# The masked-product inverse of a linear-attention chunk: turning by VectorE in place of TensorE products

## The chip, the cores and the metric

One Trainium2 chip, one of its NeuronCores. The metric is the device time of one execution in microseconds. A core has five engines with queues of their own: TensorE (PE: matmuls, with PEld loading weights), VectorE (DVE), ScalarE (ACT), GpSimd (POOL) and SyncE (SP, here the queue of the weight loads). They are kept in order by semaphores that the kernel waits on by hand.

## What is computed

A decoder trunk of two layers on 512 tokens of width 1024, all in float32. Layer 0 has a feed-forward block, a mixer (sliding-window attention beside RWKV-7), a second feed-forward block and a gated embedding; layer 1 the same with forgetting attention. Only the RWKV-7 part of layer 0 is touched by the change. It has 8 heads of width 64, and the reference runs it token by token:

```python
def step(state, inp):
    r_t, w_t, k_t, v_t, kk_t, a_t = inp
    s_kk = jnp.einsum('bhij,bhj->bhi', state, kk_t)
    state = (state * w_t[:, :, None, :]
             - s_kk[..., None] * (kk_t * a_t)[:, :, None, :]
             + v_t[..., None] * k_t[:, :, None, :])
    return state, jnp.einsum('bhij,bhj->bhi', state, r_t)
```

## The kernel before

The kernel works in chunks of C = 64 tokens (NC = 8 chunks). Within a chunk the recurrence becomes products with the inverse of a unit triangular 64x64 matrix, I + A, where A is made of the masked products of `b` and `kk`. There are 8 heads x 8 chunks = 64 such matrices. They are treated in two passes, `h` = 0 and `h` = 1 (heads 0 to 3, heads 4 to 7), and each pass in two halves, `q` = 0 and 1. A half is one 128x512 tile: two matrices on top of each other (64 partitions each), eight side by side. So one operation of VectorE, GpSimd or ScalarE on a half is 128x512, and one "group" of TensorE is 16 products 64x64x64 in float32, which the profile shows as 32 instructions.

The inverse grows by doubling: level 0 inverts blocks of 2x2, then each level 1 to 5 (LEVELS = 6) doubles the blocks. Both the inverse M (`m_x[:, q, 0]`) and its transpose (`mt_inv`) are kept, since TensorE contracts over the partitions. One level is:

- `a_level` (GpSimd, L2462): the part of A that this level joins, `a_lev = am0 * mask`.
- `xs` (TensorE, through the helper at L1894): X = the product of `a_lev` and M, one group a half.
- `x_copied` (ScalarE, L2126): X from PSUM to `m_x[:, q, 1]`.
- `ms` (TensorE): `mx`, the correction of M, and `mxt`, the correction of its transpose, one group each a half. At level 5 only `mxt`.
- `level_done` (VectorE, L2263 and L2268): `m_x[:, q, 0] -= mx`, `mt_inv -= mxt`.

The start of a pass: `ab` and `ak` (TensorE, L1881) make the pair products; `ab_masked` (VectorE, L2230) writes `am0` and `am2`, `ak_masked` (L2243) writes `akm`. Then TensorE turns `am0` by products with `eye` (`aab`), VectorE masks the result from PSUM (L2252) and subtracts it from the unit matrix (L2256): M of level 0. GpSimd makes the transposed start from `am0` alone (L2440, L2444) and then `diag` (L2451). `f` (TensorE, needs `akm`) is copied by ScalarE (`f_copied`, L2119).

Each engine's order is written out by hand. Between the levels of pass 0 stands the front of pass 1 (`front[0]` to `front[10]`): `lora_w` (its bank is freed by `f_copied`), the sigmoid `sig_w` with a table load (L1703), the scan `lc` (L1747), `lcm` (L1751), and so on; also `late[0]`, two mixes (L1496). Between the levels of pass 1 stands the tail of pass 0: `yz` (TensorE, waits for both `f_copied` of pass 1), `y_raw` (L2297), `gn_squared`, `gn_summed` (L2309), `g` (L2035), `g_copied`, `gn_std` with a table load (L2171), `gn_normed` (L2320), `y_turned`, `y_weighted`, `y_lows` (L2336). Behind the last level come `w_and_e`, `gq`, `hs`, `yc`, and the chain of states.

The helper `seen` makes an engine wait for the step of that name, pass and half; `level_seen` the same for a level; `turn_seen` for steps whose halves come in the other order in pass 0.

Of the kernel before, what the change touches and what calls it, by code (L numbers as in the profile page):

```python
# [71 lines left out]
    "pair_products": "ab ak aab f", "pair_masks": "ab_masked ak_masked init m0", "inverse_start": "mt_masked mt0 diag",  # L72
    "f_copied": "f_copied", "a_level": "a_level", "x": "x", "x_copied": "x_copied", "mx": "mx", "mxt": "mxt",
# [32 lines left out]
def trunk(nc, dram, out, stages=STAGES):  # L106

    ctx = ExitStack()
    with ctx:
# [165 lines left out]
        masks = view("masks", [P, 9, C])  # L275
# [924 lines left out]
        rwkv_fills = 56  # L1200
# [374 lines left out]
        MASK_T, MASK_TI, MASK_0, MASK_LT = 0, 1, 2, 3  # L1575
# [290 lines left out]
        def rwkv_tensor(pe, st):  # L1866
# [68 lines left out]
            def aab(h):  # L1935
                for q in range(2):
                    turn_seen(pe, "ab_masked", h, q)
                    tokens_to_tokens(rb(q, 0), [(lambda j, t: am0[h][t, q, j], lambda j, t: eye[t])]
                                     ).then_inc(R["aab"], 1)

# [6 lines left out]
            def xs(h, level):  # L1947
                for q in range(2):
# [5 lines left out]
                    tokens_to_tokens(rb(q, 2), [(lambda j, t: a_lev[t, q, j], lambda j, t: m_x[t, q, 0, j])]  # L1954
                                     ).then_inc(R["x"], 1)

            def ms(h, level):
                for q in range(2):
# [5 lines left out]
                    if level + 1 < LEVELS:  # L1964
                        tokens_to_tokens(rb(q, 3), [(lambda j, t: mt_inv[t, q, j], lambda j, t: m_x[t, q, 1, j])]
                                         ).then_inc(R["mx"], 1)
                    else:
                        pe.sem_inc(R["mx"], 1)
                    tokens_to_tokens(rb(q, 0), [(lambda j, t: m_x[t, q, 1, j], lambda j, t: mt_inv[t, q, j])]
# [79 lines left out]
            aab(0)  # L2049
            f(0)  # L2050
            front[0]()
            xs(0, 1)
# [30 lines left out]
            aab(1)  # L2083
            f(1)
            xs(1, 1)
# [28 lines left out]
        def rwkv_scalar(act, st):  # L2114
# [6 lines left out]
            def x_copied(h, level):  # L2121
                for q in range(2):
                    level_seen(act, "x", h, level, q)
                    if level > 1:
                        level_seen(act, "mxt", h, level - 1, q)
                    nc.scalar.copy(m_x[:, q, 1], by_chunk(rb(q, 2)[:])).then_inc(R["x_copied"], 1)  # L2126
# [53 lines left out]
            front[0]()  # L2180
            f_copied(0)
            front[1]()
            x_copied(0, 1)
# [12 lines left out]
            yc_copied(0)  # L2196
            f_copied(1)
            x_copied(1, 1)
# [925 lines left out]
```

## Time and profile before

| | |
|---|---|
| median of 3 runs | 2134.8 us (2132.43 to 2135.35) |
| the profiled execution | 2133.81 us, its span 2131.9 us |
| TensorE busy | 2090.7 us, 98% of the span |
| VectorE busy | 1437.8 us, 67% |
| ScalarE busy | 849.9 us, 40% |
| GpSimd busy | 751.3 us, 35% |
| matmuls over L1894 in the chain of waits | 3% of the span |

The two passes of the inverse with what stands between them run from 511 to about 647 us of the span. A timeline row is: start, duration, engine, line, operation, output<-input, count, and in brackets the idle time of the engine before it with what ended it. Several like instructions in a row are merged; they overlap a little, so a merged duration is less than the sum. The row of a group of instructions by line gives the shortest, median and longest duration in ns. Granted clock 1.00 is 2.4 GHz, 0.50 is 1.2 GHz.

### The profile page before, as it was taken

Reading aid. Unit: us, or ns where it says so; the run is one execution under the profiler, and the core shown is the slowest. Engines: PE = TensorE matmul, PEld = TensorE weight load, DVE = VectorE, ACT = ScalarE, POOL = GpSimd, SP = SyncE. Lnnn points to the kernel's source line nnn. Section 1 sums busy time; section 2 is a strip of 40 time slices with the busy share of each in tenths; the row PEclk is TensorE's granted clock in tenths of the full one; section 3 lists DMA queues with packets and bytes.
Section 4 is the critical chain, followed back from the end, with each engine's and each line's share of the span. In section 5 each row is a group of like instructions: output and inputs, shape, how many; then the busy total and the mean of one; then the engine's idle time right before and its main releaser. Section 6 shows DMA issues by size and latency. Waiting matters only on the chain.

```text
span 2131.9 us, 37887 instructions
## 1 busy us (share of the span) xinstructions
PE 2090.7 (98%) x15232; PEld 1811.5 (85%) x15232; DVE 1437.8 (67%) x1748; ACT 849.9 (40%) x1152; POOL 751.3 (35%) x646
## 2 busy tenths in 40 slices
PE   8999999999989999999999999999999999999998
PEld 7989898777887899999788899987776689998977
DVE  7847576679756865656778575766666677575764
ACT  6434243454233433333344342434444344343434
POOL 2233244547433223233443141433333322323343
PEclk9999999999999999999999999999999999999999
DMA  5333333321003333343343343424323232433332
GB/s 159 89 109 103 101 86 88 89 61 40 4 4 100 99 90 109 92 117 85 96 116 89 92 117 89 119 70 111 88 79 89 79 99 80 119 88 107 89 93 89
DMA packets 366507, 192.95 MB, mean 91 GB/s; under 512 B 11038, under 2 KB 363408, under 8 KB 366368
## 3 DMA queue, kind: packets, MB, share of 16 engines
q1 hardware_dynamic: 364128, 185.11, 30.9%
q0 software_dynamic: 2224, 5.86, 0.9%
q8 instruction: 103, 1.69, 0.3%
q14 instruction: 36, 0.29, 0.0%
q10 hardware_dynamic: 16, 0.00, 0.0%
HBM read 188.81 MB, written 2.13 MB: 90 GB/s over the span
## 4 chain that ended last, share of the span: by engine, by line
PE 88%; DVE 7%; ACT 2%; issue 1%; DMA 0%; POOL 0%; ACTq 0%; DVEq 0%; SPq 0%; POOLq 0%
PE bank L468 13%; PE bank L470 13%; PE bank L469 12%; PE bank L633 11%; PE bank L634 11%; PE bank L635 11%; PE bank L1894 3%; PE bank L2544 2%; DVE w_lo L458 2%; PE bank L2546 2%; PE bank L2545 2%; PE bank L1246 1%; PE bank L1248 1%; PE bank L1247 1%; PE bank L2561 1%
## 5 line engine op out<-in xcount | busy, mean ns | idle before, releaser
L458 DVE TENSOR_TENSOR w_lo<-w_raw,w_hi 128x2048 fp32r<-128x2048 f32 (+3 forms) x192 | 393.3, 2049 | 137.9 <-ACT w_hi L453 136.9
L453 ACT CAST w_hi<-w_raw 128x2048 fp32r<-128x2048 f32 (+3 forms) x192 | 281.6, 1467 | 386.7 <-PE bank L635 164.8
L619 POOL TENSOR_TENSOR sums<-w_raw 128x512 f32<-128x512 f32 x68 | 94.9, 1395 | 778.5 <-DMA w_raw<-in_ffn_w_gu_dram 521.6
L468 PE MATMUL bank<-h_hi,w_hi 128*128 128x512 f32 x704 | 275.4, 391 | 2.2 <-DVE w_lo L458 1.9
L469 PE MATMUL bank<-h_hi,w_lo 128*128 128x512 f32 x704 | 274.2, 389 | 0.0
L470 PE MATMUL bank<-h_lo,w_hi 128*128 128x512 f32 x704 | 274.0, 389 | 0.0
L975 DVE SCALAR_TENSOR_TENSOR x<-bank,x 128x512 f32<-128x512 f32 (+1 forms) x96 | 66.3, 690 | 166.8 <-PE bank L470 166.1
L468 PEld LDWEIGHTS bank<-h_hi,w_hi 128*128 128x128 f32 x704 | 132.2, 188 | 35.0 <-issue 5.2
L633 PE MATMUL bank<-t_hi,s_hi 128*128 128x256 f32 x544 | 154.5, 284 | 1.7 <-issue 1.7
L470 PEld LDWEIGHTS bank<-h_lo,w_hi 128*128 128x128 f32 x704 | 132.2, 188 | 27.6
L469 PEld LDWEIGHTS bank<-h_hi,w_lo 128*128 128x128 f32 x704 | 132.2, 188 | 26.3
L633 PE MATMUL bank<-xn_hi,w_hi 128*128 128x256 f32 x544 | 154.4, 284 | 0.0
L633 PE MATMUL bank<-t_hi,w_hi 128*128 128x256 f32 x544 | 154.0, 283 | 0.0
L634 PE MATMUL bank<-t_hi,w_lo 128*128 128x256 f32 x544 | 154.0, 283 | 0.0
L635 PE MATMUL bank<-t_lo,s_hi 128*128 128x256 f32 x544 | 153.9, 283 | 0.0
L634 PE MATMUL bank<-xn_hi,w_lo 128*128 128x256 f32 x544 | 153.9, 283 | 0.0
L635 PE MATMUL bank<-t_lo,w_hi 128*128 128x256 f32 x544 | 153.9, 283 | 0.0
L634 PE MATMUL bank<-t_hi,s_lo 128*128 128x256 f32 x544 | 153.9, 283 | 0.0
L635 PE MATMUL bank<-xn_lo,w_hi 128*128 128x256 f32 x544 | 153.9, 283 | 0.0
L468 PE MATMUL bank<-xn_hi,w_hi 128*128 128x512 f32 x328 | 129.6, 395 | 1.6 <-DVE w_lo L458 1.0
L470 PE MATMUL bank<-xn_lo,w_hi 128*128 128x512 f32 x328 | 127.7, 389 | 0.0
L469 PE MATMUL bank<-xn_hi,w_lo 128*128 128x512 f32 x328 | 127.7, 389 | 0.0
(388 smaller groups left out, 5455.9 us busy)
## 6 DMA issues: line engine op xcount, KB each, us to landing
w_raw<-in_ffn_w_gu_dram SPq DMA_DIRECT2D x176, 512.0 KB, 5.1
w_raw<-in_ffn_w_down_dram SPq DMA_DIRECT2D x128, 256.0 KB, 3.1
w_raw<-in_ffn_w_down_dram SPq DMA_DIRECT2D x64, 192.0 KB, 3.2
w_raw<-in_even_w_in_dram SPq DMA_DIRECT2D x40, 256.0 KB, 3.3
w_raw<-in_ple_w_gate_dram SPq DMA_DIRECT2D x16, 512.0 KB, 3.7
w_raw<-in_fox_w_in_dram SPq DMA_DIRECT2D x16, 512.0 KB, 5.0
w_raw<-in_even_w_out_dram SPq DMA_DIRECT2D x16, 256.0 KB, 3.6
w_raw<-in_fox_w_in_dram SPq DMA_DIRECT2D x16, 256.0 KB, 4.3
```

The costliest lines, as they stand in the source:

```text
L453: nc.scalar.copy(w_hi[slot][:, 0:tiles], w_raw[slot][:, 0:tiles]).then_inc(w_hi_ready, 1)
L458: nc.vector.tensor_tensor(w_lo[slot][:, 0:tiles], w_raw[slot][:, 0:tiles], w_hi[slot][:, 0:tiles].bitcast(F32), ALU.subtract).then_inc(w_r ...
L468: nc.tensor.matmul(dst, w[0], hi[:, k], start=k == 0, stop=False)
L469: nc.tensor.matmul(dst, w[1], hi[:, k], start=False, stop=False)
L470: last = nc.tensor.matmul(dst, w[0], lo[:, k], start=False, stop=k == tiles - 1)
L619: nc.gpsimd.tensor_tensor(sums[:, 0:4], w[:, 8:12], w[:, 12:16], ALU.add).then_inc(sums_made, 1)
L633: nc.tensor.matmul(dst, w[0][:, k], b[0][:, k], start=k == 0, stop=False)
L634: nc.tensor.matmul(dst, w[1][:, k], b[0][:, k], start=False, stop=False)
L635: last = nc.tensor.matmul(dst, w[0][:, k], b[1][:, k], start=False, stop=k == 3)
L975: return nc.vector.scalar_tensor_tensor(x[:, ds(j)], bank[2 * slot][:], 0.5, x[:, ds(j)], ALU.mult, ALU.add)
L1894: mm = nc.tensor.matmul(dst[of_chunk(c), at:at + C], lhsT(j, of_chunk(c)), rhs(j, of_chunk(c)), start=k == 0, stop=k == len(operands) - 1)
L2544: nc.tensor.matmul(dst, hi, xn_hi[:, k], start=k == 0, stop=False)
```

## The change

TensorE no longer turns `am0`, and `mx` is no longer computed. VectorE makes `mt_inv` of level 0 from `am0` (mask, subtract), and M from `mt_inv` by a transpose in 32x32 blocks, at the start and behind the subtraction of levels 1 to 4. Up to there every block of M that isn't zero lies in a 32x32 block on the diagonal. GpSimd loses `start_inverse`, and one mask goes with its six fills. `xs` and `ms` change banks. In the hand-written orders `start_inverse` comes ahead of `ak_masked` on VectorE, `xs(h, 1)` ahead of `f` on TensorE, and `x_copied(h, 1)` ahead of `f_copied` on ScalarE.

```diff
-            def aab(h):
-                for q in range(2):
-                    turn_seen(pe, "ab_masked", h, q)
-                    tokens_to_tokens(rb(q, 0), [(lambda j, t: am0[h][t, q, j], lambda j, t: eye[t])]
-                                     ).then_inc(R["aab"], 1)
...
-                    tokens_to_tokens(rb(q, 2), [(lambda j, t: a_lev[t, q, j], lambda j, t: m_x[t, q, 0, j])]
+                    tokens_to_tokens(rb(q, 0), [(lambda j, t: a_lev[t, q, j], lambda j, t: m_x[t, q, 0, j])]
...
-                    if level + 1 < LEVELS:
-                        tokens_to_tokens(rb(q, 3), [(lambda j, t: mt_inv[t, q, j], lambda j, t: m_x[t, q, 1, j])]
-                                         ).then_inc(R["mx"], 1)
-                    else:
-                        pe.sem_inc(R["mx"], 1)
-                    tokens_to_tokens(rb(q, 0), [(lambda j, t: m_x[t, q, 1, j], lambda j, t: mt_inv[t, q, j])]
+                    tokens_to_tokens(rb(q, 2), [(lambda j, t: m_x[t, q, 1, j], lambda j, t: mt_inv[t, q, j])]
...
-            aab(0)
+            xs(0, 1)
             f(0)
             front[0]()
-            xs(0, 1)
...
-            aab(1)
+            xs(1, 1)
             f(1)
-            xs(1, 1)
             yz(0, 0)
...
             front[0]()
+            x_copied(0, 1)
             f_copied(0)
             front[1]()
-            x_copied(0, 1)
...
+            x_copied(1, 1)
             f_copied(1)
-            x_copied(1, 1)
...
+            def blocks_turned(q):
+                return nc.vector.transpose(m_x[:, q, 0].rearrange("p j t -> p (j t)"),
+                                           mt_inv[:, q].rearrange("p j t -> p (j t)"))
...
             def start_inverse(h):
                 for q in range(2):
-                    seen(dve, "aab", h, q)
+                    turn_seen(dve, "ab_masked", h, q)
                     if h:
                         seen(dve, "yc", 0, q)
-                    nc.vector.tensor_tensor(m_x[:, q, 1], by_chunk(rb(q, 0)[:]), over_chunks(masks[:, MASK_0]),
-                                            ALU.mult).then_inc(R["init"], 1)
-                for q in range(2):
-                    seen(dve, "init", h, q)
-                    nc.vector.tensor_tensor(m_x[:, q, 0], over_chunks(eye[:]), m_x[:, q, 1], ALU.subtract
-                                            ).then_inc(R["m0"], 1)
+                    nc.vector.tensor_tensor(mt_inv[:, q], am0[h][:, q], over_chunks(masks[:, MASK_LT]), ALU.mult
+                                            ).then_inc(R["mt_masked"], 1)
+                for q in range(2):
+                    seen(dve, "mt_masked", h, q)
+                    nc.vector.tensor_tensor(mt_inv[:, q], over_chunks(eye[:]), mt_inv[:, q], ALU.subtract
+                                            ).then_inc(R["mt0"], 1)
+                for q in range(2):
+                    seen(dve, "mt0", h, q)
+                    blocks_turned(q).then_inc(R["m0"], 1)
 
             def level_done(h, level):
                 for q in range(2):
+                    level_seen(dve, "mxt", h, level, q)
+                    if level == 1:
+                        seen(dve, "mt0", h, q)
+                    nc.vector.tensor_tensor(mt_inv[:, q], mt_inv[:, q], by_chunk(rb(q, 2)[:]), ALU.subtract
+                                            ).then_inc(R["mt"], 1)
+                    level_seen(dve, "mt", h, level, q)
                     if level + 1 < LEVELS:
-                        level_seen(dve, "mx", h, level, q)
-                        nc.vector.tensor_tensor(m_x[:, q, 0], m_x[:, q, 0], by_chunk(rb(q, 3)[:]), ALU.subtract
-                                                ).then_inc(R["m"], 1)
-                    level_seen(dve, "mxt", h, level, q)
-                    if level + 1 == LEVELS:
+                        blocks_turned(q).then_inc(R["m"], 1)
+                    else:
                         dve.sem_inc(R["m"], 1)
-                    nc.vector.tensor_tensor(mt_inv[:, q], mt_inv[:, q], by_chunk(rb(q, 0)[:]), ALU.subtract
-                                            ).then_inc(R["mt"], 1)
...
             ab_masked(0)
+            start_inverse(0)
             ak_masked(0)
-            start_inverse(0)
             late[0]()
...
             ab_masked(1)
+            start_inverse(1)
             ak_masked(1)
-            start_inverse(1)
...
             a_level(0, 1)
-            start_inverse(0)
             diag(0)
...
             a_level(1, 1)
-            start_inverse(1)
             diag(1)
```

## Rows read from the trace of the kernel before

**Rows 1.** The page: each engine's busy us, share of the span, instructions.
```profile
PE 2090.7 (98%) x15232; PEld 1811.5 (85%) x15232; DVE 1437.8 (67%) x1748; ACT 849.9 (40%) x1152; POOL 751.3 (35%) x646
```
**Rows 2.** Stretches of 10 us in pass 0 and pass 1; columns in the first line.
```profile
core 0: us, PE busy (x) PEld busy (x) DVE busy (x) ACT busy (x) POOL busy (x), PEclk, DMA share, GB/s
...
535.00:545.00 10.00, 10.00 (x228) 9.92 (x227) 10.00 (x18) 1.43 (x3) 6.18 (x5) 0.79 0.01 2
...
595.00:605.00 10.00, 10.00 (x372) 10.00 (x363) 7.08 (x13) 2.68 (x5) 6.54 (x6) 1.00 0.02 5
```
**Rows 3.** Timeline of VectorE at the start of pass 0; columns as told above.
```profile
515.77 2.47 DVE L2243 TENSOR_TENSOR akm<-bank,masks 128x512 f32<-128x512 f32 x4
518.16 1.27 DVE L2252 TENSOR_TENSOR m_x<-bank,masks 128x512 f32<-128x512 f32 x2
519.36 2.52 DVE L2256 TENSOR_TENSOR m_x<-eye,m_x 128x512 f32<-128x512 f32 x2
...
525.16 2.06 DVE L1747 TENSOR_TENSOR_SCAN act_in<-chunk_start,kr 128x512 f32<-128x512 f32 x1
...
529.06 1.69 DVE L1751 TENSOR_TENSOR kr<-act_in,kr 128x512 f32<-128x512 f32 x1
```
**Rows 4.** Timeline of TensorE in pass 0: `aab`, `f`, and `xs` of level 2.
```profile
515.93 2.06 PE L1894 MATMUL bank<-eye,am 64*64 64x64 f32 x64
517.82 2.03 PE L1894 MATMUL bank<-vtok,akm 64*64 64x64 f32 x64
...
533.17 3.68 PE L1894 MATMUL bank<-m_x,a_lev 64*64 64x64 f32 x64 [2.58 <-DVE m_x L2263]
```
**Rows 5.** Timeline of VectorE at the start of pass 1.
```profile
587.31 2.47 DVE L2243 TENSOR_TENSOR akm<-bank,masks 128x512 f32<-128x512 f32 x4
```
**Rows 6.** Timeline of TensorE in pass 1: last `ab`/`ak`, then `xs` and `ms`.
```profile
583.53 1.98 PE L1881 MATMUL bank<-kr,bk 64*64 64x128 f32 x64 [0.20 <-DVE am L2290]
...
591.90 1.15 PE L1894 MATMUL bank<-m_x,a_lev 64*64 64x64 f32 x32 [0.92 <-DVE m_x L2256]
...
598.73 2.00 PE L1894 MATMUL bank<-m_x,a_lev 64*64 64x64 f32 x62
...
601.06 1.13 PE L1894 MATMUL bank<-m_x,mt_inv 64*64 64x64 f32 x32
...
604.80 2.06 PE L1894 MATMUL bank<-m_x,a_lev 64*64 64x64 f32 x64
```
**Rows 7.** The chain that ended last, pass 1: start, length, what.
```profile
609.41 1.28 ACT L2171
...
624.84 0.69 DVE mt_inv L2268
```
**Rows 8.** Instructions by line, VectorE: shortest, median, longest ns, starts.
```profile
L2268 DVE TENSOR_TENSOR mt_inv<-mt_inv,bank x20: 672/678/689, 532.9 to 625.4; 128x512 f32<-128x512 f32 x20
...
L1757 DVE TENSOR_SCALAR bk<-tmp,vecs x4: 471/473/1261, 478.2 to 537.5; 128x512 f32<-128x512 f32 x4
```
**Rows 9.** Timeline of GpSimd: two maskings, two subtractions, two of `diag`.
```profile
515.93 2.50 POOL L2462 TENSOR_TENSOR a_lev<-am,masks 128x512 f32<-128x512 f32 x2 [1.61 <-DVE am L2230]
...
521.30 3.40 POOL L2444 TENSOR_TENSOR mt_inv<-eye,mt_inv 128x512 f32<-128x512 f32 x2
...
594.52 2.05 POOL L2451 TENSOR_TENSOR kr<-eye,chunk_end 128x512 f32<-128x512 f32 x2
```
**Rows 10.** Timeline of ScalarE behind `f_copied` of pass 0.
```profile
520.50 1.28 ACT L1703 ACT_TABLE_LOAD   x1
```
**Rows 11.** Timeline of TensorE: its longest other wait in the stage.
```profile
658.01 0.50 PE L468 MATMUL bank<-y_hi,w_hi 128*128 128x512 f32 x1 [3.04 <-DVE y_lo L2336]
```
**Rows 12.** Stretches of 1 us where the clock came back (columns as rows 2).
```profile
538.00:539.00 1.00, 1.00 (x25) 1.00 (x24) 1.00 (x1) 0.00 (x0) 1.00 (x1) 0.50 0.00 0
539.00:540.00 1.00, 1.00 (x35) 1.00 (x34) 1.00 (x2) 0.00 (x0) 1.00 (x2) 0.86 0.07 16
...
662.00:663.00 1.00, 1.00 (x6) 0.84 (x5) 0.94 (x2) 0.79 (x1) 0.22 (x1) 0.92 0.94 249
```

More of the change, by code:

```diff
@@ L71 @@
     "front_tails": "a_decayed b_tail k_tail masks_scaled",
-    "pair_products": "ab ak aab f", "pair_masks": "ab_masked ak_masked init m0", "inverse_start": "mt_masked mt0 diag",
-    "f_copied": "f_copied", "a_level": "a_level", "x": "x", "x_copied": "x_copied", "mx": "mx", "mxt": "mxt",
+    "pair_products": "ab ak f", "pair_masks": "ab_masked mt_masked mt0 m0 ak_masked", "diag": "diag",
+    "f_copied": "f_copied", "a_level": "a_level", "x": "x", "x_copied": "x_copied", "mxt": "mxt",
     "m": "m", "mt": "mt",
@@ L274, in trunk @@
         swa_rcp = view("swa_rcp", [P, 2, NB])
-        masks = view("masks", [P, 9, C])
+        masks = view("masks", [P, 8, C])
         eye = view("eye", [P, C])
@@ L1199, in trunk @@
         FIRST_WINDOW, APART = 27, 22
-        rwkv_fills = 56
+        rwkv_fills = 50
         hb_diff = [(prod, act_out, sq, sq_sum)[i] for i in (0, 1, 2, 3, 0, 1, 2, 3, 2, 3, 0, 1)]
@@ L1573, in chunk_seen @@
             e.wait_ge(R[name], 2 * (h * (NC - first) + c - first) + q + 1)
-        MASK_T, MASK_TI, MASK_0, MASK_LT = 0, 1, 2, 3
+        MASK_T, MASK_TI, MASK_LT = 0, 1, 2
         def turn_seen(e, name, h, q):
@@ L2125, in x_copied @@
                         level_seen(act, "mxt", h, level - 1, q)
-                    nc.scalar.copy(m_x[:, q, 1], by_chunk(rb(q, 2)[:])).then_inc(R["x_copied"], 1)
+                    nc.scalar.copy(m_x[:, q, 1], by_chunk(rb(q, 0)[:])).then_inc(R["x_copied"], 1)
             def we_copied(h):
@@ L2422, in rwkv_constants @@
                 select(m, ALU.is_ge, -k, [[0, blocks], [1, 2 * k]], 0)
-            m = masks[:, MASK_0].rearrange("p (b t) -> p b t", t=2)
-            select(m, ALU.is_ge, -1, [[-2, C // 2], [0, 2]], 1)
-            select(m, ALU.is_ge, 1, [[2, C // 2], [0, 2]], -1)
-            select(m, ALU.is_ge, 0, [[0, C // 2], [-1, 2]], 0)
             assert filled[0] == rwkv_fills
@@ L2433, in rwkv_pool @@
         def rwkv_pool(pool, st):
-            def start_inverse(h):
-                for q in range(2):
-                    turn_seen(pool, "ab_masked", h, q)
-                    if h:
-                        seen(pool, "we", 0, q)
-                    nc.gpsimd.tensor_tensor(mt_inv[:, q], am0[h][:, q], over_chunks(masks[:, MASK_LT]), ALU.mult
-                                            ).then_inc(R["mt_masked"], 1)
-                for q in range(2):
-                    seen(pool, "mt_masked", h, q)
-                    nc.gpsimd.tensor_tensor(mt_inv[:, q], over_chunks(eye[:]), mt_inv[:, q], ALU.subtract
-                                            ).then_inc(R["mt0"], 1)
             def diag(h):
```

## The prediction

> **What bounds the kernel now.** Read the page first: TensorE is busy for 98% of the span [rows 1], so a matmul saved looks like time saved. That share is an average, so the second view is the table of stretches over the inverse (511 to 625 us, both passes; pass 0 handles heads 0 to 3, pass 1 heads 4 to 7). In pass 0 TensorE and VectorE are both busy for all 10 us; in pass 1 TensorE is, VectorE for 7.1 of 10 [rows 2]. The timelines then say who waits. At the start of each pass it is VectorE: it runs without a hole from 511 to 562 us (the rows between those of [rows 3]), and TensorE fills its wait with the turning (`aab`) and with `f` [rows 4]. From 533 to 564 us the two are nearly tied. In pass 1 VectorE again sets the start [rows 5]; then TensorE is nearly continuous from one level to the next [rows 6], except where the normalisation of pass 0 (through ScalarE and VectorE) and later its `y_lows` stand ahead on VectorE [rows 7]. All that is gained or lost there moves the end of the stage, since nothing of the next stage's bulk can run before.
>
> **What is removed.** TensorE loses `aab` (64 instructions, 1.9 us in each pass [rows 4]) and `mx` of levels 1 to 4: two groups of 32 at 0.94 us, so 1.87 us a level, 7.5 us a pass (four groups make the 3.73 us from the start of `ms` to the next `xs`, 601.06 to 604.80 in [rows 6]). Together 18.8 us of its busy time. GpSimd loses four operations a pass, about 6 us (the two subtractions 3.40 us, two maskings like those of `a_level` 2.50 us [rows 9]). The six mask fills fewer lie near 360 us, with TensorE full; I cost them at nothing.
>
> **The new operation.** No 32x32 turning by VectorE is in this trace. It reads 128x512 from one place and writes as many. The nearest rows are the subtractions it replaces, 0.68 us [rows 8]; below stands the one-input TENSOR_SCALAR of L1757 at 0.47 us [rows 8], above the scan at 2.0 us [rows 3]. I take 0.68, since the subtraction is the operation nearest in form and size, and keep 0.47 and 2.0 for the range. Issued back to back such an operation costs 0.60 us, but the turning needs the subtraction just ahead of it complete, so the pair costs 0.68 + 0.68. The Trainium skill ("Vector Engine (DVE) Microarchitecture Reference", section 3.8) says that the transposing front end sustains one element per cycle and lane; no run here shows that yet, and by it my value would stand.
>
> **The start is the dear part.** VectorE's first step took the product from PSUM (0.675 us each, L2252) and one subtraction on SBUF. Now the masking reads `am0` and `masks`, both in SBUF, like the subtraction. What such an operation costs beside a busy GpSimd is in [rows 3]: the two of L2256 took 2.52 us, the two of L1751 3.4 us, against 1.27 us for the two of L2252; and in [rows 9] two of GpSimd's on this shape take 2.05 us alone and 3.40 us beside L2256. They look as if they took turns, instruction by instruction. The Trainium skill ("GPSIMD Engine Reference", section 1) says the two engines contend when VectorE has two SBUF inputs; the rows agree. The turning has one input and would be spared. `a_level` and `diag` of GpSimd still run here, so four operations of 0.58 us alternate with four of GpSimd of 1.25, 1.25, 1.04 and 1.04 us, of which about three fall between: 4 x 0.58 + 3.3 = 5.6 us (bounds 2.4 clear, 7.0 at L2256's longest). Then two turnings, 1.3 us, and only now `ak_masked`, 2.4 us [rows 5]. So `ak_masked` ends 9.3 us after `ab_masked`; before it ended after 2.4 us, and the start of the inverse after 6.1 us.
>
> **Pass 0.** `ab_masked` ends at 515.8. `xs(0,1)` can start at 522.4 (before: 521.7). `ak_masked` ends at 525.4, so `f` ends at 526.4 at the full clock; then `f_copied`, `lora_w`, the table load of 1.28 us that stands behind `f_copied` on ScalarE [rows 10], and the sigmoid: the scan `lc` could start at 529.1 us, and it started at 525.16. So 3.9 us of wait appear on VectorE, where none was. Then there is relief: GpSimd, 4 operations shorter, is out of the way when the two of L1751 run (3.3 us become 1.2): -2.1. Net +1.8 us when VectorE reaches level 1. From there it is VectorE's own list that counts: the same 2 operations a half and level, the pair 0.1 us longer (8 pairs, +0.8), and +0.5 at level 5, where `b_turned` is behind a later `xs`. That is +3.1 us. The 5.6 us of matmuls saved in levels 2 to 4 buy nothing, since VectorE was full there and stays so.
>
> **Pass 1.** The four plus two operations end at 594.2, the first turning at 593.6; `xs(1,1)` starts at 593.7, before at 591.90. But `f` now runs behind it and needs `ak_masked` (596.6), `yz(0,0)` waits for both `f_copied`, and `ms(1,1)` is queued behind `yz(0,0)` on TensorE. At full clock `f` ends at 597.7, the copy at 598.4, `yz` at 599.0, the first product of `ms` at 600.0; subtraction and turning bring `xs(1,2)` to 601.5 against 598.73 [rows 6]: +2.8. Level 2 to 3: `xs` to `x_copied` to `ms` to the pair now runs one after the other; VectorE also has `y_raw` and `gn_summed` ahead of the pair: 6.75 us for 6.07, +0.7. Level 3 to 4: the old period is `g`, table load, `gn_normed`, then the subtraction [rows 7]; `xs` of the second half waits for its turning, and the turning is behind the subtraction: +0.95. Level 4 to `w_and_e`: here the old period was TensorE's and 1.9 us go, but `y_weighted` and `y_lows`, still ahead of the last subtraction, start later: net -0.6. Sum +3.9.
>
> **The clock.** TensorE's granted clock falls twice in the whole old trace, from 2.4 to 1.2 GHz (1.00 to 0.50), both times in or just behind a wait: 2.58 us [rows 4] and 3.04 us [rows 11]. It came back 5.8 and 4.1 us after work resumed [rows 12]; the 64 matmuls that met it took 3.68 us, not 2.0 [rows 4]. With `aab` gone and `f` moved, TensorE has nothing from 516.1 to 522.4 us in pass 0, and from 585.5 (end of `ak`, [rows 6]) to 593.7 in pass 1: 6.3 and 8.2 us. So I expect both to cost. Pass 0: `xs` 3.8 us, then `f` to 528.8; the scan starts at 531.8, not 529.1, +2.7, of which I keep 2.5. Pass 1: `xs` to 597.2, `f` to 600, `yz` to 601.3, so `xs(1,2)` at 603.75: +2.2 more. A third hole, 616.6 to 620 us, opens before `xs(1,4)`: +1.4. The clock thus adds 6.1 us: 5.6 in pass 0 and 7.5 in pass 1 in all. The Trainium skill ("TensorE: Matmul & The Clock Gate", Part 1) has idling throttle the array and activity release it, which speaks against taking filler matmuls away; the rows agree.
>
> **Sum.** 13.1 us on the profiled execution of 2133.8 us (span 2131.9) gives 2146.9; that execution is 1.0 us under the median of the three runs, 2134.8, so 2147.9 us, said as 2148.
>
> **Rivals.** (1) The clock holds, or its cost hides behind VectorE: +7.0, 2142 us. For it: pass 0 has slack on TensorE; against it, the two falls. (2) The turning is dear. At 1.2 us, ten turnings in pass 0 (VectorE full) cost 5 us more and seven on pass 1's path 4 us: 2157; at the scan's 2.0 us 2170. Only the replaced row's likeness speaks against it. (3) The other side: TensorE's queue is what each level waits for. The chain of waits goes over matmuls from 595 to 609 us and from 613 to 622 us, and over nearly all of 533 to 564. If VectorE gets from a product to the next `xs` in less than the 1.87 us that the removed products took, and the masked steps are near their clear price of 0.6 us, the savings stand: 7.5 us in pass 1 and 5.6 in pass 0, 2122 us. The point that decides is whether VectorE has idle time ahead of each level; it had in pass 1, not in pass 0. (4) Gain and loss cancel: turning near 0.47 us, GpSimd out of step with the masked steps (-3 us a pass), no low clock: 2134.
>
> **How the numbers follow.** Forecast (clock falls, turning 0.68 us) 0.48; rival 1 0.17; rival 2 0.13; rival 3 0.14; rival 4 0.08. A comparison of this kernel tells about 0.2% (4.3 us) from no change; the forecast and rivals 1 and 2 lie above it: less a hundredth at the edge of rival 1, slower 0.77; most of rival 4 and that edge, same 0.08; rival 3 and a rest of rival 4, faster 0.15. The range leaves out rival 3's centre and the upper part of rival 2: 2131 to 2163; the forecast alone would be 2142 to 2154.
>
> **What would show it.** The turnings in the profile at 0.6 to 0.75 us each; TensorE idle for 6 and 8 us ahead of the first `xs` of each pass, with a clock of 0.50 behind it; VectorE waiting some 4 to 6 us for the sigmoid before the first scan of pass 0; `xs(1,2)` some 5 us later within its pass; the time from the first `ab_masked` to `w_and_e` longer by about 6 and 7 us. I am wrong if GpSimd no longer slows VectorE at the start, if the turning's time is far from 0.68 us, or if VectorE had room in pass 0 that the trace doesn't show.

## The result and the profile after

| | kernel before | changed kernel |
|---|---|---|
| median of 6 executions | 2134.76 us (2132.43 to 2137.49) | 2145.07 us (2142.78 to 2145.98) |
| ratio to before | 1 | 1.0043, 95% interval 1.0033 to 1.0053 |
| span of the profiled execution | 2131.9 us | 2143.5 us |

The change makes the kernel 10.3 us slower by the medians; the ratio gives 9.2 us (7.0 to 11.3). Forecast were 13.1 us. It takes 18.8 us of matmuls off TensorE and still loses. The page of the changed kernel (columns as in [rows 1]):

```profile
PE 2079.7 (97%) x14592; PEld 1799.0 (84%) x14592; DVE 1437.8 (67%) x1752; ACT 849.6 (40%) x1152; POOL 736.5 (34%) x632
```

All 640 matmuls are gone, but busy time fell by 11.0 us only: the rest of the 18.8 came back as matmuls at half clock. VectorE's total is the same to the tenth by chance: in the stage it is 2.8 us more (94.6 for 91.8), since the new operations are dearer, and behind the stage, on code that the change leaves alone, it is 2.8 us less (988.4 for 991.1). The stretches of the changed kernel over pass 0, pass 1 and one of [rows 2], columns in the first line:

```profile
core 0: us, PE busy (x) PEld busy (x) DVE busy (x) ACT busy (x) POOL busy (x), PEclk, DMA share, GB/s
511.00:575.00 64.00, 49.78 (x1206) 42.97 (x1208) 53.61 (x74) 22.49 (x42) 27.59 (x20) 0.92 0.01 3
575.00:640.00 65.00, 46.53 (x1362) 43.17 (x1354) 37.99 (x73) 16.74 (x34) 20.02 (x16) 0.89 0.01 3
...
595.00:605.00 10.00, 7.55 (x174) 7.47 (x176) 4.64 (x8) 2.35 (x4) 2.91 (x3) 0.61 0.01 2
```

TensorE, full in 595 to 605 us before [rows 2], is busy for 7.55 of 10 us at a mean clock of 0.61, and VectorE for 4.64 where it had 7.08: each has time in which it waits for the other. VectorE at the start of pass 0, in the timeline of the changed kernel (start, length, what; in brackets the idle time ahead and who ended it), answers to [rows 3]:

```profile
515.83 2.36 DVE L2243 TENSOR_TENSOR mt_inv<-am,masks 128x512 f32<-128x512 f32 x2
518.11 3.19 DVE L2247 TENSOR_TENSOR mt_inv<-eye,mt_inv 128x512 f32<-128x512 f32 x2
521.23 1.29 DVE L2212 STREAM_TRANSPOSE m_x<-mt_inv 128x512 f32<-128x512 f32 x2
522.45 2.44 DVE L2234 TENSOR_TENSOR akm<-bank,masks 128x512 f32<-128x512 f32 x4
...
531.17 1.22 DVE L1747 TENSOR_TENSOR_SCAN act_in<-chunk_start,kr 128x512 f32<-128x512 f32 x1 [3.52 <-ACT kr L1703]
532.31 1.20 DVE L1747 TENSOR_TENSOR_SCAN other<-chunk_start,kr 128x512 f32<-128x512 f32 x1
533.43 0.67 DVE L1751 TENSOR_TENSOR kr<-act_in,kr 128x512 f32<-128x512 f32 x1
534.01 0.68 DVE L1751 TENSOR_TENSOR kr<-other,kr 128x512 f32<-128x512 f32 x1
```

The four masked steps (two of L2243, two of L2247) take 5.4 us from 515.83 to 521.23; `ak_masked` comes 6.7 us later than in [rows 3]; the scan waits 3.52 us for ScalarE's sigmoid. GpSimd beside it in the changed kernel answers to [rows 9], the two `a_level` at 1.72 us each and the two of `diag` at 1.47 us, where two of `diag` alone took 2.05 us:

```profile
515.87 3.44 POOL L2441 TENSOR_TENSOR a_lev<-am,masks 128x512 f32<-128x512 f32 x2 [1.61 <-DVE am L2221]
519.27 2.93 POOL L2430 TENSOR_TENSOR kr<-eye,chunk_end 128x512 f32<-128x512 f32 x2
```

TensorE in the timeline of the changed kernel, pass 0 and then pass 1, answers to [rows 4] and [rows 6]:

```profile
522.07 3.68 PE L1894 MATMUL bank<-m_x,a_lev 64*64 64x64 f32 x64 [6.02 <-DVE m_x L2212]
525.51 3.01 PE L1894 MATMUL bank<-vtok,akm 64*64 64x64 f32 x64
...
596.69 3.68 PE L1894 MATMUL bank<-m_x,a_lev 64*64 64x64 f32 x64 [7.81 <-DVE m_x L2212]
600.12 3.23 PE L1894 MATMUL bank<-vtok,akm 64*64 64x64 f32 x64
...
607.35 1.15 PE L1894 MATMUL bank<-m_x,a_lev 64*64 64x64 f32 x32 [0.69 <-DVE m_x L2212]
...
613.98 1.15 PE L1894 MATMUL bank<-m_x,a_lev 64*64 64x64 f32 x32 [1.83 <-DVE m_x L2212]
...
623.67 3.39 PE L1894 MATMUL bank<-m_x,a_lev 64*64 64x64 f32 x64 [3.30 <-DVE m_x L2212]
```

TensorE idles for 6.02 and 7.81 us ahead of the first `xs`, and then 64 matmuls take 3.68 us, not 2.0. The clock itself, in 1 us stretches of the changed kernel (the last column but two):

```profile
521.00:522.00 1.00, 0.00 (x0) 0.00 (x0) 1.00 (x3) 0.00 (x0) 1.00 (x1) 0.50 0.00 0
...
527.00:528.00 1.00, 1.00 (x30) 1.00 (x29) 0.65 (x1) 0.51 (x1) 0.10 (x1) 0.69 0.00 0
528.00:529.00 1.00, 1.00 (x20) 0.67 (x16) 0.00 (x0) 0.52 (x2) 0.00 (x0) 1.00 0.00 0
...
593.00:594.00 1.00, 0.00 (x0) 0.00 (x0) 1.00 (x2) 0.00 (x0) 1.00 (x2) 0.50 0.00 0
```

0.50 is 1.2 of 2.4 GHz. It fell inside the wait and came back some 5.6 us after work resumed at 522.07. It fell once more in pass 0, from 544 to 549 us behind a wait of 2.22 us; VectorE ran without a hole from 531 to 564 us, so this second fall held nothing up that VectorE's list did not.

To compare all kernels I cut the stage at four places: pass 0 and pass 1 from the first `ab_masked` of the pass to its first product of `w_and_e`; the gap between; and the tail from the second `w_and_e` to the first operation that reads `yc` of pass 1. All are read off the timelines of each profiled execution, in us; "sum" is the whole stretch against the kernel before.

| kernel | pass 0 | gap | pass 1 | tail | sum | ratio, 95% interval |
|---|---|---|---|---|---|---|
| before | 51.3 | 20.2 | 40.9 | 14.0 | 0 | 1 |
| changed | 54.9 | 20.1 | 47.3 | 16.1 | +11.9 | 1.0043 [1.0033, 1.0053] |
| levels_only | 52.5 | 22.8 | 42.3 | 14.0 | +5.2 | 1.0011 [1.0002, 1.0020] |
| start_only | 54.0 | 20.2 | 46.9 | 14.1 | +8.7 | 1.0025 [1.0016, 1.0034] |
| order_back | 50.6 | 20.4 | 43.6 | 14.4 | +2.5 | 1.0015 [1.0006, 1.0024] |
| filler | 55.5 | 20.7 | 44.7 | 13.8 | +8.2 | 1.0034 [1.0022, 1.0046] |
| diag_late | 54.0 | 19.8 | 46.7 | 14.8 | +8.9 | 1.0029 [1.0017, 1.0041] |
| turn_twice | 60.5 | 20.1 | 48.3 | 13.9 | +16.4 | 1.0068 [1.0054, 1.0082] |
| mxt_twice | 56.6 | 19.8 | 48.8 | 14.6 | +13.4 | 1.0049 [1.0036, 1.0063] |
| by_identity | 53.8 | 20.5 | 44.9 | 14.6 | +7.3 | 1.0019 [1.0010, 1.0028] |
| filled | 50.2 | 20.0 | 43.5 | 14.0 | +1.2 | 1.0007 [0.9998, 1.0016] |
| filled_again | 50.2 | 20.8 | 42.2 | 14.1 | +0.9 | 0.9993 [0.9984, 1.0002] |
| hybrid | 50.2 | 21.4 | 41.4 | 14.4 | +0.9 | 0.9994 [0.9985, 1.0003] |

A row is one execution, a ratio stands for 5 to 11. 0.0001 of the ratio is 0.21 us, and between a row's sum and its ratio lie up to 3.4 us. A part of that is known: the profiled execution of the kernel before is 1.0 us under its median, the stage begins between 512.3 and 513.6 us (513.1 before), and three of the kernels gain 1.5 us at one place behind the stage (last section). Apart from that place, what lies behind the stage is as long as before to within 0.4 us in all thirteen.

### The profile page after: what moved, and what is told of

Read it like the earlier page. It is cut to its first block, busy times and chain, and to the rows that moved or that the text cites. A ratio compares the mean times of both kernels' runs of the same rounds, so it can differ in the third digit from the quotient of the medians.

```text
span 2143.5 us, 36599 instructions
## 1 busy us (share of the span) xinstructions
PE 2079.7 (97%) x14592; PEld 1799.0 (84%) x14592; DVE 1437.8 (67%) x1752; ACT 849.6 (40%) x1152; POOL 736.5 (34%) x632
## 4 chain that ended last, share of the span: by engine, by line
PE 87%; DVE 9%; ACT 2%; issue 2%; DMA 0%; POOL 0%; ACTq 0%; DVEq 0%; SPq 0%; POOLq 0%
PE bank L468 13%; PE bank L470 12%; PE bank L469 12%; PE bank L633 11%; PE bank L635 11%; PE bank L634 11%; PE bank L2521 2%; PE bank L1894 2%; DVE w_lo L458 2%; PE bank L2523 2%; PE bank L2522 2%; PE bank L1246 1%; PE bank L1248 1%; PE bank L1247 1%; PE bank L2538 1%
```

## The experiments

**Which half of the change loses.** `levels_only` keeps the old start of each pass and turns in the levels; `start_only` is the opposite. The edit of `levels_only` against the changed kernel, with the old order and GpSimd's part written back too:

```diff
+            aab(0)
...
+                    nc.vector.tensor_tensor(m_x[:, q, 1], by_chunk(rb(q, 0)[:]), over_chunks(masks[:, MASK_0]),
+                                            ALU.mult).then_inc(R["init"], 1)
```

The edit of `start_only`, `mx` written back into the levels:

```diff
+                        tokens_to_tokens(rb(q, 3), [(lambda j, t: mt_inv[t, q, j], lambda j, t: m_x[t, q, 1, j])]
+                                         ).then_inc(R["mx"], 1)
...
+                        nc.vector.tensor_tensor(m_x[:, q, 0], m_x[:, q, 0], by_chunk(rb(q, 3)[:]), ALU.subtract
+                                                ).then_inc(R["m"], 1)
```

> Only the levels are changed: mx is left out and VectorE turns mt_inv behind its subtraction in levels 1 to 4; the start of each pass (aab, the two masked steps from PSUM, GpSimd's part, the order of f) is as in the kernel before. Theory (the start of each pass is what costs; in the levels the 15 us of matmuls saved buy almost nothing and the turning costs almost nothing): pass 0 +1 to +1.5 us, pass 1 about 0, so 2135 to 2138 us, 0 to 3 us over the kernel before. Rival A (the pair of subtraction and turning is the cost): 2142 us or more. Rival B (TensorE's queue is what the levels wait for, and only the start hides it): 2125 us or less.

> Only the start of each pass is changed (VectorE makes the masked steps alone, the inverse is turned by VectorE ahead of the products with m_x, no work of GpSimd or TensorE in between); in the levels m_x lies in the bank beside the inverse as in the kernel before. It closes the sum: levels alone gave +2.6 us, the start undone took 6.4 us off the changed kernel. If the parts add up, the time is 2141 to 2145 us (about +7 to +8 us, ratio 1.0033 to 1.0038), with TensorE at half clock behind the masked steps in both passes and pass 1 some 5 us longer than before. Rival (the loss is made in the levels, and the start costs little by itself): 2137 us or less, ratio under 1.0015.

Measured 2137.72 us (ratio 1.0011, +2.4 us) and 2141.45 us (1.0025, +5.3 us). The two add up to 7.7 us, inside the 7.0 to 11.3 us of the whole. `levels_only` lies in its range of times, though its pass 1 is 1.3 us longer, where about 0 had been expected. `start_only` lies in its range of times but under its range of ratios; its passes are 2.7 and 5.9 us longer, where some 5 us had been expected of pass 1, and TensorE is at half clock behind the masked steps of both. So most of the loss is the start of a pass, and the levels, which shed 15 us of matmuls, lose 2.4 us by themselves; in the profiled execution they lose 1.2 us in pass 0 and 1.3 in pass 1.

**Which part of the start.** `order_back` leaves VectorE's masked steps and puts only the order back: `ak_masked`, then the start of the inverse; `f`, then `xs`; `f_copied`, then `x_copied`.

```diff
             ab_masked(0)
-            start_inverse(0)
             ak_masked(0)
+            start_inverse(0)
```

> The changed kernel with the old order at the start of each pass: ak_masked ahead of the start of the inverse on VectorE, f ahead of xs on TensorE, f_copied ahead of x_copied on ScalarE. The work is that of the changed kernel. Theory (a part of the loss is f behind the start of the inverse, and with it the sigmoid and the first scan in pass 0 and yz in pass 1): the scan starts about 3.5 us earlier, xs(1,2) some 1 to 2 us earlier, in all 4 to 5 us less than the changed kernel: 2140 to 2141 us. Rival (the order is no part of it, the first xs sets everything, and it comes 2.4 us later in each pass): 2147 us or more.

Measured 2138.66 us, ratio 1.0015: 6.0 us of the changed kernel's 9.2 are gone (0.0028 of 2135), more than the 4 to 5 us I had expected. The timeline of `order_back`, VectorE and then TensorE:

```profile
518.24 2.26 DVE L2243 TENSOR_TENSOR mt_inv<-am,masks 128x512 f32<-128x512 f32 x2
520.42 2.13 DVE L2247 TENSOR_TENSOR mt_inv<-eye,mt_inv 128x512 f32<-128x512 f32 x2
...
524.98 1.21 DVE L1747 TENSOR_TENSOR_SCAN act_in<-chunk_start,kr 128x512 f32<-128x512 f32 x1
```

```profile
517.18 2.34 PE L1894 MATMUL bank<-vtok,akm 64*64 64x64 f32 x64 [0.99 <-DVE akm L2234]
...
523.32 3.44 PE L1894 MATMUL bank<-m_x,a_lev 64*64 64x64 f32 x64 [1.88 <-DVE m_x L2212]
```

The scan starts without a wait, 0.2 us before that of [rows 3], and pass 0 is 0.7 us shorter than before. The clock still drops, here behind a wait of 1.88 us. What the new order costs is thus mostly the late `ak_masked`, and what hangs on it through `f` and ScalarE. A part is something else: behind `ak_masked` the four masked steps begin 2.4 us later and meet less of GpSimd's work, so that they take 4.2 us, not 5.4. The order was put back on three engines at once; no run separates them.

The profiled execution is one of four near 2135.6 us; the other seven of `order_back` lie from 2138.3 to 2140.9 us. Its row in the table stands for those four, and no trace shows where the others lose 3 to 5 us more.

**What the clock costs.** `filler` leaves the order and the steps of the changed kernel, and gives TensorE 3 x 64 products while it waits for VectorE; nobody reads them, and they lie in the bank that `xs` overwrites.

```diff
+            def filler(h):
+                for n in range(3):
+                    for q in range(2):
+                        if n == 0:
+                            turn_seen(pe, "ab_masked", h, q)
+                        tokens_to_tokens(rb(q, 0), [(lambda j, t: am0[h][t, q, j], lambda j, t: eye[t])])
...
+            filler(0)
             xs(0, 1)
```

> The changed kernel with TensorE kept busy in the wait ahead of the first xs of each pass: three times the removed turning by products with eye, into a bank that xs then overwrites; nobody waits for it. Theory (the low clock behind the idle 6 and 8 us is part of the loss): the granted clock stays 1.00 at both starts, the 64 matmuls of xs take 2.0 us and not 3.7, the scan of pass 0 starts 2 us earlier and xs(1,2) 2 us earlier: 2141 us, 4 less than the changed kernel. Rival (VectorE covers the slow matmuls): 2145 us, no change though the clock is 1.00.

Measured 2143.27 us, 1.0034: 1.9 us back, not 4. At both starts the clock stayed at 1.00, the scan came 2.4 us earlier and pass 1 got 2.6 us shorter. But pass 0 did not (55.5 us for 54.9): the clock fell some microseconds further on, and in all three times, near 530, 543 and 560 us, where the changed kernel's fell twice. The timeline of `filler`, TensorE, and its stretches of 2 us:

```profile
526.53 1.98 PE L1637 MATMUL bank<-th,lora_wa 64*128 64x512 f32 x4
529.29 2.99 PE L1644 MATMUL bank<-th,lora_wa 64*128 64x512 f32 x4 [0.77 <-ACT kr L1703]
532.21 3.68 PE L1894 MATMUL bank<-mt_inv,m_x 64*64 64x64 f32 x64
```

```profile
528.00:530.00 2.00, 1.23 (x4) 0.43 (x3) 0.73 (x1) 1.80 (x3) 0.00 (x0) 1.00 0.00 0
530.00:532.00 2.00, 2.00 (x3) 0.38 (x2) 2.00 (x3) 0.69 (x1) 0.00 (x0) 0.53 0.03 8
```

No idle time beyond 0.77 us stands before this fall. So filler in the longest hole can move the fall instead of removing it. The 2.6 us of pass 1 are what the clock cost at its start, against the 2.2 us of the forecast. What it costs pass 0 this run does not isolate, since the clock was low there for longer than in the changed kernel.

**GpSimd beside the masked steps.** `diag_late` holds GpSimd's `diag` back until VectorE has turned.

```diff
+                    seen(pool, "m0", h, q)
```

> The changed kernel with GpSimd's diag put behind the first turning by a wait, so that of GpSimd's work only a_level runs beside the four masked steps of VectorE. Theory (VectorE's steps with two SBUF inputs and GpSimd's operations take turns): the two subtractions from eye take 1.3 us in all and not 3.0 to 3.2, each pass starts 1.8 us earlier, in all 3 to 4 us less than the changed kernel: 2141 to 2142 us. Rival (the steps are slow by themselves, for instance by their broadcast operand): they stay at 3.0 us and the time at 2145 us.

Measured 2141.77 us, 1.0029, as forecast in the time, 3.0 us less than the changed kernel. But the passes of its profiled execution are only 0.9 and 0.6 us shorter; another 1.3 us is the tail, where the clock fell in the changed kernel's profiled execution and not in this one. In the timeline of `diag_late` the two subtractions of pass 0 take 2.35 us, where 1.3 had been expected and the changed kernel had 3.19; those of pass 1 take the 1.3:

```profile
518.36 2.35 DVE L2247 TENSOR_TENSOR mt_inv<-eye,mt_inv 128x512 f32<-128x512 f32 x2
...
592.10 1.28 DVE L2247 TENSOR_TENSOR mt_inv<-eye,mt_inv 128x512 f32<-128x512 f32 x2
```

GpSimd in the timeline of pass 0:

```profile
516.12 3.43 POOL L2442 TENSOR_TENSOR a_lev<-am,masks 128x512 f32<-128x512 f32 x2 [1.61 <-DVE am L2221]
521.41 2.04 POOL L2431 TENSOR_TENSOR kr<-eye,chunk_end 128x512 f32<-128x512 f32 x2 [1.85 <-DVE m_x L2212]
```

`a_level` alone, until 519.55 us, still meets three of the four steps; in pass 1 it ends at 591.6 us, before the subtractions begin. That it is the neighbour and not the operation is seen for all four steps in `filled_again` (below), where `a_level` is over by 587.9 us; timeline of VectorE, and of GpSimd:

```profile
588.86 1.28 DVE L2254 TENSOR_TENSOR mt_inv<-am,masks 128x512 f32<-128x512 f32 x2
590.06 1.28 DVE L2258 TENSOR_TENSOR mt_inv<-eye,mt_inv 128x512 f32<-128x512 f32 x2
```

```profile
585.30 2.61 POOL L2453 TENSOR_TENSOR a_lev<-am,masks 128x512 f32<-128x512 f32 x2 [10.35 <-DVE am L2232]
592.04 2.04 POOL L2442 TENSOR_TENSOR kr<-eye,chunk_end 128x512 f32<-128x512 f32 x2 [4.14 <-DVE m_x L2223]
```

The same four steps take 2.5 us here and 5.4 us in the changed kernel, and GpSimd's two 2.61 us in place of 3.44. The Trainium skill ("GPSIMD Engine Reference", section 1) names VectorE instructions with two SBUF inputs as those that contend with GpSimd; this agrees, and so does the turning, with one input, which took 1.29 us for two in the changed kernel, with GpSimd busy beside it until 522.2 us.

**Does VectorE's list set pass 0, or TensorE's?** Two kernels double one thing each in pass 0: `turn_twice` the turning of levels 1 to 4, into a tile about to be overwritten (eight turnings, each behind the subtraction), `mxt_twice` the product `mxt` of the same levels (256 matmuls). First the one, then the other:

```diff
+                        if h in (0,):
+                            nc.vector.transpose(m_x[:, q, 1].rearrange("p j t -> p (j t)"),
+                                                mt_inv[:, q].rearrange("p j t -> p (j t)"))
...
+                    if h in (0,) and level + 1 < LEVELS:
+                        tokens_to_tokens(rb(q, 2), [(lambda j, t: m_x[t, q, 1, j], lambda j, t: mt_inv[t, q, j])])
```

> The changed kernel with each of the 8 turnings in the levels of pass 0 made twice, the first time into a place that nobody reads. Theory (in pass 0 VectorE's own list sets the end, TensorE has room): 8 x 0.64 us, so pass 0 is 5 us longer, 2150 us. It also gives the price of a dearer turning. Rival (TensorE or the clock sets pass 0): 0 to 2 us longer, 2145 to 2147 us.

> The changed kernel with the products mxt of levels 1 to 4 of pass 0 made twice, the second over the first: 7.5 us more of matmuls, as many as mx took from pass 0 before. Theory (the matmuls taken out of pass 0 bought nothing): pass 0 within 1 us of the changed kernel, 2144 to 2146 us, and shorter rather than longer, since the clock then falls less. Rival (each removed matmul counts, and the loss elsewhere hides it): 5 to 7 us longer, 2150 us or more.

`turn_twice`: 2149.95 us, 1.0068. The timeline of `turn_twice`, the added turning and the one behind it:

```profile
535.93 0.71 DVE L2263 STREAM_TRANSPOSE m_x<-mt_inv 128x512 f32<-128x512 f32 x1
536.57 0.67 DVE L2212 STREAM_TRANSPOSE m_x<-mt_inv 128x512 f32<-128x512 f32 x1
```

VectorE's next operation starts at 537.16 us, so the two take 1.23 us where one took 0.63 (535.33 to 535.96 us in the changed kernel). The added turnings thus lengthen VectorE's list by 8 x 0.60 = 4.8 us; the median rose by 4.9 us and pass 0 of the one profiled execution by 5.7.

`mxt_twice`: 2145.34 us, 1.0049; 7.5 us more of TensorE's work brought 1.7 us in the pass of its one profiled execution and 0.3 us in the median (within 1 us had been expected of the pass); the two ratios differ by 1.3 us. So in pass 0 each microsecond of VectorE counts in full, and of TensorE's a quarter at most: the matmuls taken off it there could buy little.

**A way without VectorE's subtraction.** `by_identity` lets TensorE add the inverse to `mxt` in the bank through the identity, in pass 0, and ScalarE copy the sum out, so that VectorE has only the turning.

```diff
+                    if h == 0:
+                        parts.append((lambda j, t: eye[t], lambda j, t: mt_inv[t, q, j]))
...
+                    nc.scalar.copy(mt_inv[:, q], by_chunk(rb(q, 2)[:])).then_inc(R["mt"], 1)
```

> As filled, and in pass 0 the sum is made by TensorE: X is copied with a minus sign, mxt also adds mt_inv by products with eye, ScalarE copies the sum from PSUM to mt_inv, and VectorE only turns. VectorE loses 10 subtractions of pass 0 (6 us), TensorE gets 9.4 us back. Theory (VectorE's list sets pass 0): pass 0 shorter by 3 to 5 us than in filled, down to where TensorE is full again, 2128 to 2131 us, under both kernels. Rival (TensorE's list is nearly as long, so nothing is won): 2132 us or more.

A miss: 2139.38 us, 1.0019, and pass 0 at 53.8 us where its base, with VectorE's subtraction (`filled`), had 50.2. The timeline of `by_identity`, TensorE and VectorE:

```profile
536.80 0.48 PE L1894 MATMUL bank<-mt_inv,m_x 64*64 64x64 f32 x4 [2.88 <-ACT m_x L2123]
```

```profile
541.06 0.71 DVE L2233 STREAM_TRANSPOSE m_x<-mt_inv 128x512 f32<-128x512 f32 x1 [2.21 <-ACT mt_inv L2129]
```

VectorE now waits 2.21 us for ScalarE's copy, and TensorE 2.88 us for another. The level became one chain through three engines, and in these two waits taking VectorE's operation away only made ScalarE the one that is waited for. Another place for the copies in ScalarE's order was not tried.

**Does anything beat the kernel before?** `filled` is `order_back` with TensorE's holes filled and `diag` late; `filled_again` splits the filler of pass 1 in two, right behind `ab_masked` and behind `f`; `hybrid` leaves pass 1 as it was before the change, and in pass 0 keeps the products of `aab` as its filler.

`filled` adds a filler ahead of `xs(0,1)`, a double one ahead of `xs(1,1)` and one at level 4 of pass 1:

```diff
+            filler(0, 1)
             xs(0, 1)
...
+            filler(1, 2)
             xs(1, 1)
...
+            filler(1, 1)
             xs(1, 4)
...
+                    seen(pool, "m0", h, q)
```

`filled_again` against `filled`:

```diff
+            for q in range(2):
+                turn_seen(pe, "ab_masked", 1, q)
+            filler(1, 1)
             f(1)
-            filler(1, 2)
+            filler(1, 1)
```

`hybrid` against `filled`; `aab` and GpSimd's start of the inverse stand in pass 1 again too:

```diff
+                    if h and level + 1 < LEVELS:
+                        tokens_to_tokens(rb(q, 3), [(lambda j, t: mt_inv[t, q, j], lambda j, t: m_x[t, q, 1, j])]
+                                         ).then_inc(R["mx"], 1)
```

> The changed kernel with the old order at the start of each pass, GpSimd's diag behind the first turning, and TensorE kept busy by products that nobody reads ahead of xs(0,1) (64 instructions), xs(1,1) (128) and xs(1,4) (64). Theory (what order_back still loses against the kernel before is the low clock and the turns taken with GpSimd, mostly in pass 1): pass 0 about 50 us, pass 1 40 to 41 us, 2132 to 2134 us, at or just under the kernel before. Rival (the rest is the longer path from a product over subtraction and turning to the next xs): no change against order_back, 2138 to 2139 us.

> As the kernel with TensorE's holes filled by products that nobody reads, but in pass 1 the long filler stands in two parts, right behind ab_masked and behind f, so that it does not overrun the first product with m_x. Theory (the clock is the loss of pass 1, and the filler of before overran by some 2.5 us): pass 1 takes 41 to 41.5 us from ab_masked to w_and_e where the first filled kernel took 43.5, and the time is 2133 to 2135 us, level with the kernel before (ratio 0.9990 to 1.0002). Rival (the masked steps of VectorE without help set the start, filler or not): pass 1 stays at 43 us or more, ratio 1.0005 or more.

> Pass 1 entirely as in the kernel before; pass 0 with VectorE's start and turning, the old order of the products around it and the holes of TensorE filled. The filled kernel took 50.2 us for pass 0 where the kernel before took 51.3. Theory (the gain of pass 0 is there to be had by itself): 50.2 us again, pass 1 at 40.9 us, the time 2133 to 2134.2 us (ratio 0.9991 to 0.9999). Rival (the 1.1 us of pass 0 are given back in the gap between the passes or in pass 1): ratio 1.0000 or more.

`filled`: 2135.89 us, 1.0007, over its forecast. Pass 0 is 1.1 us shorter than before, but the filler of pass 1 met the low clock and overran; timeline of `filled`, TensorE:

```profile
590.14 4.92 PE L1894 MATMUL bank<-eye,am 64*64 64x64 f32 x128
594.90 1.98 PE L1894 MATMUL bank<-m_x,a_lev 64*64 64x64 f32 x62
```

The turned inverse had been there since 592.2 us. `filled_again` took the overrun away: `xs` starts 8.5 us after `ab_masked`, not 11.4, and the ratio is 0.9993 [0.9984, 1.0002], the median 2134.54 us against 2135.8 us of the kernel before, measured beside it. It is as expected in the time, but pass 1 took 42.2 us, over the 41 to 41.5 expected: another drop of the clock followed at level 3, behind a wait of 1.66 us. `hybrid` gave 2134.18 us, 0.9994 [0.9985, 1.0003], with pass 0 at 50.2 and pass 1 at 41.4 us; the 1.1 us won in pass 0 went again in the gap between the passes (21.4 for 20.2) and in pass 1 (0.5); in its profiled execution TensorE stood for 1.31 us within its own queue near 570 us, where the kernel before stood for 0.17, which is the whole of the gap's growth; no work was added there, and why the queue stood longer is open. Both are level with the kernel before; neither beats it beyond what is measured.

## Why the prediction was right, point by point

**The bound.** Right: VectorE is what pass 0 waits for, by `turn_twice` and `mxt_twice`. The 7.5 us of `mx` in pass 0 bought nothing, as forecast.

**The turning.** 0.68 us were taken, between 0.47 and 2.0. The instructions by line of the changed kernel (ns, shortest, median, longest):

```profile
L2212 DVE STREAM_TRANSPOSE m_x<-mt_inv x20: 662/711/714, 521.2 to 630.1; 128x512 f32<-128x512 f32 x20
```

0.711 us, of which 0.64 us lie ahead of the next start. The replaced subtraction was the right row to go by, and rival 2 is out. The Trainium skill ("Vector Engine (DVE) Microarchitecture Reference", section 3.8) gives the transposing front end the rate of one element per cycle and lane; the row does not speak against it, since the turning costs 5% more than a subtraction of the same size, but no run here measures the rate itself.

**The masked steps.** 5.6 us forecast, 5.4 us measured, by the mechanism named: they are slow beside GpSimd. The first `xs` came 9.0 us after the start of `ab_masked` for 9.3, and in pass 1 8.7 us for 9.0. `by_identity` (1.41 and 1.28 us for the two pairs) and `filled_again` show the price without GpSimd, 2.5 to 2.6 us, close to the lower bound of 2.4.

**Pass 0: +5.6 forecast, +3.6 measured.** The scan started at 531.17 us, forecast 531.8: nearly right, and its wait of 3.52 us is the sigmoid's (4 to 6 us had been named as the sign). The term that was mis-sized is the relief, -2.1 us. I counted it for the two of L1751 only, and took the scans at their 2 us of [rows 3] as their own price. But they too had been held up: alone they take 1.22 and 1.20 us. Scans and L1751 together took 7.2 us from 525.16 us before and take 3.4 us after, 3.8 us less where 2.1 were counted: 1.7 us of the 2.0 missing. What is left is the start of the scan, +6.0 us where 3.9 + 2.5 were put. The pairs and level 5 came out as forecast: +1.3 us from the first subtraction of level 1 to the end of the pass, for 0.8 + 0.5.

**Pass 1: +7.5 forecast, +6.4 measured.** From `ab_masked` to `xs(1,2)` +5.2 us (forecast 5.0); to `xs(1,3)` 6.6 us for 6.1, +0.6 (0.7); to `xs(1,4)` 9.7 for 8.5, +1.2 (0.95); from there to `w_and_e` 11.6 for 12.2, -0.6, where -0.6 and the clock's +1.4 had been put. The clock's 1.4 us is the term that was mis-sized, it came to nothing: the third hole came (3.30 us of wait, then `xs` in 3.39 us), the clock fell, and yet `xs(1,5)` followed 6.2 us behind `xs(1,4)`, before 7.0. The slower `xs` was absorbed by the matmuls that are no longer there.

**What was not forecast.** The tail grew by 2.1 us in the profiled execution. TensorE stood for 1.91 us within its own queue near 643.8 us (1.36 us at the same products before), and the clock fell behind it; the stretches of the changed kernel:

```profile
646.00:647.00 1.00, 1.00 (x44) 1.00 (x40) 0.16 (x2) 0.65 (x2) 0.00 (x0) 1.00 0.00 0
...
648.00:649.00 1.00, 1.00 (x24) 1.00 (x22) 0.00 (x0) 0.59 (x1) 0.00 (x0) 0.50 0.00 0
```

`turn_twice`, with the same tail in its code, took 13.9 us there and `mxt_twice` 14.6, so not every execution of this code has it. That the profiled sum, 11.9 us, lies above the 10.3 us of the medians has another reason: the profiled execution of the changed kernel is its median one, that of the kernel before is 1.0 us under its median.

A part of the forecast's nearness is luck. The passes were put 3.1 us too high (2.0 and 1.1), and a tail that nobody had forecast gave 2.1 us of it back in the execution that was profiled. Of the 6.1 us put down to the clock, the runs bear out the 2.2 us at the start of pass 1 (2.6), and not the 1.4 us at its third hole (0); the 2.5 us of pass 0 are seen at the scan (2.4), but `filler` did not turn them into a shorter pass.

Two readings of the old trace in the prediction were off, without weight in the sum: the clock came back 6.1 us after work resumed at 533.17 us, not 5.8, and it falls a third time, at 2130 us, in the last 2 us of the span.

**The rivals.** That the clock holds (2142 us) is out for the changed kernel, whose clock fell at both starts. What it would gain if the clock held throughout is not shown: `filler`, with the clock up at the starts and low elsewhere, gave 2143.27. That TensorE's queue sets each level (2122 us) is out by `mxt_twice` for pass 0; in pass 1 something is in it, since `w_and_e` came 0.6 us sooner from `xs(1,4)`, but not 7.5 us. That gain and loss cancel (2134) was reached only with the order put back, `diag` late and the holes filled.

**Open.** How much of the 2.4 us of `levels_only` is the passes and how much the gap is not settled. In its profiled execution the gap is 2.6 us longer (22.8 for 20.2): TensorE stands there for 0.95 and 1.82 us within its own queue, for 0.17 and 1.55 before, and the clock falls behind it; the passes and the gap together, 5.2 us, are more than the ratio bears out. What the low clock costs pass 0, and which of the three orders that `order_back` put back counts most, is open too. A start in which `a_level` is held back as well was not tried for the order of the changed kernel.

## What to carry to other kernels

Read an operation's price beside its neighbours: an instruction of VectorE with two SBUF inputs cost 1.2 to 1.6 us beside GpSimd and 0.64 without, and the same was hidden in the scans' row of before, where a fall of GpSimd's load gives back more than the one line one looks at. A product that TensorE makes while it waits anyway costs little (7.5 us of them cost at most 1.7 us in `mxt_twice`), and its removal can open a hole: check the granted clock on both sides before counting matmuls as saved. When an operation is moved up on an in-order engine, follow the one that it passes to its last reader: here putting the order back took off 6.0 of 9.2 us, with every new operation left in.

## What the runs showed of the hardware that was not expected

**The clock's fall is not settled by the wait ahead of it.** Each of the thirteen kernels has the wait of [rows 11], 3.04 us long before y_lo's products. In ten of the profiled executions the clock fell behind it, in three not. The changed kernel (fell) and `start_only` (held), timeline and stretches of 4 us from about the same point:

```profile
669.85 0.50 PE L468 MATMUL bank<-y_hi,w_hi 128*128 128x512 f32 x1 [3.04 <-DVE y_lo L2331]
```

```profile
669.00:673.00 4.00, 3.15 (x10) 2.48 (x11) 3.23 (x5) 1.99 (x4) 0.32 (x1) 0.75 0.99 286
673.00:677.00 4.00, 4.00 (x16) 3.26 (x15) 2.76 (x4) 2.11 (x4) 1.30 (x2) 0.83 0.94 248
```

```profile
665.94 0.50 PE L468 MATMUL bank<-y_hi,w_hi 128*128 128x512 f32 x1 [3.04 <-DVE y_lo L2337]
```

```profile
665.00:669.00 4.00, 3.06 (x13) 2.42 (x14) 3.23 (x5) 2.11 (x4) 0.34 (x1) 1.00 0.87 248
669.00:673.00 4.00, 4.00 (x20) 3.27 (x19) 2.76 (x4) 2.11 (x4) 1.29 (x2) 1.00 1.01 274
```

The three that held (`start_only`, `filled_again`, `hybrid`) are 1.5 us shorter behind the stage than the others, all of it in the 95 us behind that wait, on the same products. So one chance fall is worth 1.5 us, and a difference of a single pair of spans should not be read for less; it is a part of why a span and a median differ by 1 to 3 us, as far as one profiled execution of each kernel can say. The Trainium skill ("TensorE: Matmul & The Clock Gate", Part 1) says that the number of matmuls at the low clock at a kernel's start varies from run to run of one kernel; no run here repeats one kernel under the profiler, but the traces show the same of the fall, between kernels with the same code at that place.

**It also falls behind short waits**: of 2.22 us in the changed kernel, 1.88 us in `order_back`, 1.66 us in `filled_again`, and 0.77 us around four long matmuls on 64 rows in `filler`. A filler into the one hole that is seen does not hold it by itself.

**VectorE's scan, which reads two tiles in SBUF, is slowed beside GpSimd too**: 1.22 and 1.20 us alone for 128x512 in the changed kernel, beside GpSimd 2.06 us in the kernel before and 2.22 us for the second scan of `order_back`.
